# Hybrid mLSTM and short-convolution step: row operations in pieces inside the next pair, convolution ahead of the gates, chunks in two passes, four sums stored

## What is computed

```
xn = rmsnorm(x, norm_w)
q, k, v, i, f, o, z_m, b_g, c_g, x_c, z_c, g_m, g_c = split(xn @ w_in)      # 1024 x 10248
h  = mlstm_chunkwise(q, k * DQK**-0.5, v, i + b_i, log_sigmoid(f + b_f), C0, n0, m0)
h  = h * rsqrt(mean(h*h) + EPS) * head_norm_w
y_m = (h * sigmoid(o) * silu(z_m)) @ w_proj_m
y_c = (silu(z_c) * b_g * short_conv(c_g * x_c, conv0, conv_w)) @ w_proj_c
y  = rmsnorm(x + (sigmoid(g_m) * y_m + sigmoid(g_c) * y_c) @ w_out, final_norm_w)
```

## Time and profile before

| | us |
|---|---|
| three runs | 2537.21, 2540.91, 2544.01 (median 2540.91) |
| the profiled execution | 2534.89 |
| its span, first to last instruction | 2533.1 |
| TensorE busy in it | 2386.8 (94%) |
| DVE busy | 1556.8 (61%) |
| ACT busy | 886.8 (35%) |
| GpSimd busy | 95.2 (4%) |

### The profile page before, as it was taken

How to read it: one execution, slowest core, us unless ns; L and a number is a source line. 1 busy time by engine, 2 the same in 40 slices (tenths; PEclk the granted TensorE clock), 3 DMA queues, 4 the chain that set the end, 5 groups by cost and what they waited for, 6 DMA issues and landing times. The chain is left out here.

```text
span 2533.1 us, 42100 instructions
## 1 busy us (share of the span) xinstructions
PE 2386.8 (94%) x14825; PEld 2303.0 (91%) x14825; DVE 1556.8 (61%) x2792; ACT 886.8 (35%) x1613; POOL 95.2 (4%) x82
## 2 busy tenths in 40 slices
PE   7997998999998889999999899999998999999998
PEld 7996997999998889899999899998998999999886
DVE  4334777778887878666777766666776523333333
ACT  4223443443333434444344444443343301001111
POOL 0003000000000000000100000000000000000000
PEclk9998998999999889999999999999999999999999
DMA  6444766787755567566544446575542743335452
GB/s 208 125 125 130 266 201 220 248 241 225 255 198 195 177 234 229 188 208 197 187 154 160 145 159 209 173 220 171 145 155 103 257 154 110 99 95 173 126 148 84
DMA packets 303537, 449.50 MB, mean 177 GB/s; under 512 B 27226, under 2 KB 250586, under 8 KB 289622
## 3 DMA queue, kind: packets, MB, share of 16 engines
q1 hardware_dynamic: 303446, 448.31, 55.4%
HBM read 293.13 MB, written 155.16 MB: 177 GB/s over the span
## 5 line engine op out<-in xcount | busy, mean ns | idle before, releaser
L1453 PE MATMUL b_g<-x_hi,w_hi 128*128 128x344 f32 (+1 forms) x3024 | 999.3, 330 | 67.8 <-DVE part L1128 30.0
L1453 PE MATMUL b_g<-x_lo,w_hi 128*128 128x344 f32 (+1 forms) x3024 | 976.8, 323 | 0.0
L1453 PE MATMUL b_g<-x_hi,w_lo 128*128 128x344 f32 (+1 forms) x3024 | 974.7, 322 | 0.0
L1453 PEld LDWEIGHTS b_g<-x_hi,w_hi 128*128 128x128 f32 x3024 | 578.8, 191 | 81.9 <-DVE part L1128 29.3
L1453 PEld LDWEIGHTS b_g<-x_lo,w_hi 128*128 128x128 f32 x3024 | 579.2, 192 | 2.0
L1453 PEld LDWEIGHTS b_g<-x_hi,w_lo 128*128 128x128 f32 x3024 | 578.6, 191 | 0.0
L976 ACT ACTIVATE w_hi<-w_operands 128x512 fp32r<-128x512 f32 x533 | 332.9, 629 | 494.1 <-PE b_g L1453 488.1
L1095 DVE TENSOR_TENSOR w_lo<-w_operands,w_hi 128x512 fp32r<-128x512 f32 x533 | 373.3, 705 | 0.8 <-ACT w_hi L976 0.5
L1777 PE MATMUL c_g<-act_hi,RH 128*128 128x294 f32 x896 | 268.1, 299 | 11.7 <-DVE act_lo L1727 11.7
L1777 PE MATMUL c_g<-act_hi,RL 128*128 128x294 f32 x896 | 268.0, 299 | 0.0
L1777 PE MATMUL c_g<-act_lo,RH 128*128 128x294 f32 x896 | 267.5, 299 | 0.0
(11 more groups left out here) (257 smaller groups left out, 2548.7 us busy)
## 6 DMA issues: line engine op xcount, KB each, us to landing
w_operands<-w_ops_d SPq DMA_DIRECT2D x36, 1792.0 KB, 8.5
stages<-w_ops_d SPq DMA_DIRECT2D x36, 1024.0 KB, 5.1
w_ops_d<-w_operands SPq DMA_DIRECT2D x18, 1792.0 KB, 9.4
w_operands<-w_in SPq DMA_DIRECT2D x108, 256.0 KB, 4.8
w_operands<-w_ops_d SPq DMA_DIRECT2D x36, 768.0 KB, 7.3
w_ops_d<-stages SPq DMA_DIRECT2D x18, 1024.0 KB, 7.2
w_ops_d<-w_operands SPq DMA_DIRECT2D x18, 768.0 KB, 8.4
stages<-w_in SPq DMA_DIRECT2D x36, 256.0 KB, 3.7
```

The lines of the kernel that those rows point to most:

```text
L1453: last = nc.tensor.matmul(bank[:, 0:n], w[:, j, k, :], x[:, k, 0:n], start=(j < 4 and k == 0 and m == 0), stop=(k == 3 and m == 2), skip_g ...
```

## The change

Five things in phase b, and one in phase c.

1. `finish` is cut into pieces with a position `at`, and each engine issues piece j of the *previous* pair behind its step j of the current one (`ended`). The sums of the next-but-one pair move from steps 3 to 6 to steps 5 and 6 of the pair and 0 and 4 of the next. SP stores the odd pair's rows in the next body (`store_rows(*before, 1)`), and the weights after that.
2. The order is q/k, o/z, convolution, gates. The turn falls on the last gates body.
3. Chunks only in passes two (7) and three (9): convolution bodies 4 to 7, or 2 to 7, and gates 0 to 2. The decode's inputs are loaded in convolution body 1 of pass one, its rows written in body 2; four samples are updated in the o/z bodies of pass two and four in those of pass three, one per body; the next pass's x quarters are loaded in gates body 0.
4. `w_ops_d` holds the four sums only. A load in passes two and three is five transfers: three raw blocks from `w_in` and two of sums.
5. The first tap of the convolution (times `cw[2]`) and the eviction of each head's numerator go from DVE to ACT; DVE's multiplication by the head norm goes away, and phase c multiplies `w_proj_m` by it in the instructions that split it.

```diff
 def load_w(pair, p, s, i, q):                       # p > 0
-    src = g.w_ops_d[FIRST[s] + 2 * i + q]
-    for n, part in enumerate(g.W7[q]):
-        sp.dma_start(flat, src[:, 2048 * n:2048 * n + flat.shape[1]]).then_inc(w_ops_in[q], 16)
+    sp.dma_start(operand(g, q, 0), w[:, 0:4, c0:c0 + P]).then_inc(w_ops_in[q], 16)
+    sp.dma_start(operands(q, 1, 4), src[:, 0:3]).then_inc(w_ops_in[q], 16)
+    sp.dma_start(operand(g, q, 4), w[:, 4:8, c0:c0 + P]).then_inc(w_ops_in[q], 16)
+    sp.dma_start(operand(g, q, 5), w[:, 4:8, c1:c1 + P]).then_inc(w_ops_in[q], 16)
+    sp.dma_start(operand(g, q, 6), src[:, 3]).then_inc(w_ops_in[q], 16)
...
 # SP, one body
     load_w(pair + 2, *following, 0)
+    if extra == "chunk" and c not in (0, 7):
+        store_hg(c - 1)
+        load_gate(c)
+    if before:
+        store_rows(*before, 1)
     store_w(pair + 1, 1)                            # pass one
+    if extra == "chunk" and not last_chunk:
+        load_kq(c + 1)
...
     load_w(pair + 3, *following, 1)
-    store_w(pair + 2, 0)
     store_rows(p, s, i, 0)
+    store_w(pair + 2, 0)
...
-    store_rows(p, s, i, 1)
...
 # ACT, one body
     for q in range(2):
+        ended = (p, s, i, 0) if q else (*before, 1) if before else None
         for j in range(7):
             chunk(chunk_of(p, s, i), 7 * q + j)
             step(p, s, i, q, j)
-        finish(p, s, i, q)
+            if ended:
+                finish(*ended, j)                   # tanh at 0, gates' second tanh at 1
...
+    if s == "conv" and q == 0 and at == 1:
+        act.wait_ge(u_hist, 1 + 8 * p + i + 1)
+        nc.scalar.activation(CV[:, 0:n], UB[:, 2:2 + n], ACT.Copy, scale=cw[:, 2, bass.ds(i, 1)]).then_inc(cw_set, 1)
...
 def chunk(c, at):                                   # ACT, at 4, 6, 8, 10
+    act.wait_ge(den_set, NH * c + h + 1)
+    nc.scalar.activation(HB[:, h, :], PN[:, 0:DHV], ACT.Copy, scale=den[:, 1, h:h + 1]).then_inc(h_set, 1)
...
 # DVE, one body
         for j in range(7):
             extras(p, s, i, extra, 7 * q + j)
             step(p, s, i, q, j)
-            if s == "conv" and q == 1:
-                convolve(p, i, j)
-            if p == 0 and extra != "turn" and j >= 3:
-                sums(pair_of(p, s, i, q) + 2, half_of(p, s, i, q) + 1, q, j - 3)
+            if ended:
+                finish(*ended, j)
+            if p == 0 and not last_of_pass(s, i, q) and j in (0, 4):
+                sums(pair + 1, half + q, 1 - q, 2 if j == 0 else 3)
+            if p == 0 and extra != "turn" and j >= 5:
+                sums(pair + 2, half + 1, q, j - 5)
-        finish(p, s, i, q)
...
 # DVE's pieces: o/z at 1 (waits for z_set) and 2; the convolution's product at 0,
 # taps at 2, 3 and 4 (2 waits for cw_set); its three row operations at 1, 2 and 4
```

More of the change, by code:

```diff
@@ L581, in phase_b @@
[L581 to L584, removed]
+        [("qk", 0, 1, "gates_a"), ("qk", 1, 2, "gates_b"), ("oz", 0, 1, None), ("oz", 1, 4, None),
+         ("conv", 0, 1, "dec_inputs"), ("conv", 1, 2, "dec_first"), ("conv", 2, 3, "dec_rows"), ("conv", 3, 8, None),
+         ("gates", 0, 1, None), ("gates", 1, 3, None), ("gates", 3, 4, "turn")],
@@ new lines, in phase_b @@
+        [("qk", 0, 1, None), ("qk", 1, 2, None), ("oz", 0, 1, "decode"), ("oz", 1, 4, "decode"),
+         ("conv", 0, 1, None), ("conv", 1, 4, None), ("conv", 4, 8, "chunk"),
+         ("gates", 0, 1, "chunk"), ("gates", 1, 3, "chunk"), ("gates", 3, 4, "turn")],
+        [("qk", 0, 1, None), ("qk", 1, 2, None), ("oz", 0, 1, "decode"), ("oz", 1, 4, "decode"),
+         ("conv", 0, 1, None), ("conv", 1, 2, "dec_last"), ("conv", 2, 8, "chunk"),
+         ("gates", 0, 1, "chunk"), ("gates", 1, 3, "chunk"), ("gates", 3, 4, "end")]]
@@ new lines, in body @@
+                if extra == "decode":
+                    b = 4 * (p - 1) + i
+                    store_C(b)
+                    if i < 3:
+                        load_sample(b + 1)
+                if (p, s, i) in ((1, "conv", 3), (2, "conv", 1)):
+                    for par in range(2):
+                        sp.wait_ge(row_out[p][par], 1 + 16 * DMAS[p] * (2 * ROWS["qk"][par] + 4 * ROWS["oz"][par]))
+                    sp.wait_ge(state_out, 16 * (1 + 4 * p))
+                    first_loads(0 if p == 1 else 7)
@@ L1385, in extras, with body @@
                     ins.then_inc(ut_set, 1)
-            def body(p, s, i, extra):
+            def body(p, s, i, extra, before):
                 for q in range(2):
+                    ended = (p, s, i, 0) if q else (*before, 1) if before else None
+                    pair, half = pair_of(p, s, i, q), half_of(p, s, i, q)
                     for j in range(7):
@@ L1531, in extras @@
                     pe.wait_ge(dec_sq, 1)
[L1532 to L1533 removed]
+                    nc.tensor.matmul(PN[:, 0:2 * NS * NH], ones[:, :], dec[:, 3, :], start=True, stop=True).then_inc(dec_mm, 1)
+                elif extra == "end" and at == 2:
                     pe.wait_ge(c_set, HC + NH)
```

349 lines of the change are left out of this document (173 added, 176 removed).

## The result

The changed kernel takes 2467.7 us (median of four runs, 2466.9 to 2468.1) where the kernel before took 2542.0 beside it (2537.2 to 2544.0): a ratio of **0.971**, 95% interval 0.970 to 0.973. The prediction was 2472, range 2447 to 2512. The profiled execution took 2466.87 us, 68.0 less than the one of before. That the medians lie 74.3 apart is no second effect: the profile of before stood 7.1 under the 2542.0, that of after 0.8 under its own median.

The account below looks back on a forecast made before the run. Stalls of TensorE's projection products above undisturbed pairs, 140.1 us, were taken as what can be won, with VectorE late through a weight-load ring. Terms left 70.9, so 69.2 won: 2540.9 - 69.2 = 2472 us, range 2447 to 2512.

Parts of the forecast that it names:

- start: Start of the first pass: one weight sum fewer before it, stall 17.2 -> 16.5 us.
- o/z, first pass: Six o/z pairs of the first pass: earlier weight load and later sums cut the stall from 16.0 to 0.5 us.
- decode inputs: First-pass convolution body 1: TensorE waits for five loads, now also behind the row store; stall 10.7 -> 13 us.
- decode rows: First-pass convolution body 2: SP's wait for small stores delays the odd pair's load; stall 0 -> 3 us, bounds 0 and 8.
- two turns: Pass ends, now in gates pairs, where VectorE has 23 us against 13.2: both turns and q/k, 28.9 + 11.3 -> 13.0 us.
- o/z with decodes: O/z bodies of passes two and three, one decode each, late odd weights: 10.7 -> 5 and 0 -> 5 us.
- chunks: Chunk bodies of passes two and three: waits for scores and h, first loads and last decode; 5.1 + 11.4 -> 12.4 us.
- The ring: First pass: VectorE waits for the raw weight load, then late releases the next; earlier load and later sums end it.
- first loads and last decode: Part of the chunk term in passes two and three: +3 us.
- The later loads: Weight loads of passes two and three, five overlapping transfers: 10 us each, between 8.5 and 19; cover 12.8, with banks 15.2.
- slower rival: Five-part load misses quiet pairs too, lengthening all 72 pairs: +137 us, 2609 us; decides from 16.2 us of landing; 5%.
- scores late: Rival: VectorE comes late to the chunk's scores, ten convolution bodies pay 4.1 instead of 0.7 us: +34, 2506 us; 13%.

Follow-up runs that it names:

- the run with both edits undone: Changed kernel with row operations in one block behind their pair and the four weight sums early, both as before the change: 2574.7 us, ratio 1.015.
- the two single ones: Changed kernel with only the row operations in one block again (2517.6 us, ratio 0.992), and with only the four weight sums early again (2480.9 us, ratio 0.978).
- the run with the block: Changed kernel with a pair's row operations once more in one block behind its last step, in all bodies: 2517.6 us, ratio 0.992.
- the block in o/z: Changed kernel with row operations in one block behind their pair in o/z bodies alone, in pieces elsewhere: 2460.0 us, ratio 0.970.

## Why the prediction was right

The mechanism was right, and the total better than its terms: errors of both signs, 13.1 and 14.5 us, cancelled, and that is luck. By the terms 140.1 - 72.3 = 67.8 us were won where 69.2 were forecast; that the median came out 4 under the 2472 is no term of the sum. The forecast took the change from the profile off the median, as if the profile of after would lie 6.0 under its median too; it lies 0.8 under, which makes 5.2 us less, against 1.4 more in the terms. What stays, term by term as forecast and as measured from the windows above (the chunks with 1.9 of the last body):

| | forecast | measured |
|---|---|---|
| start | 16.5 | 14.8 |
| o/z, first pass | 0.5 | 0.0 |
| convolution and gates, first pass | 2.5 | 0.7 |
| decode inputs | 13 | 9.6 |
| decode rows | 3 | 0.0 |
| two turns | 13.0 | 10.9 |
| o/z with decodes | 5 + 5 | 4.4 + 5.0 |
| chunks | 12.4 | 26.9 |
| sum | 70.9 | 72.3 |

The 14.8 of the start are a matter of luck (about 17 in most of the runs). Two readings of the prediction were off, with little weight for the sum: by its own list 101.6 of the 140.1 us lay in the first pass and the turn behind it, not half, and of the two low halves stretched in the first turn only one took 3.45 us, the other 3.15.

**The ring** went as told, with slack on both sides: the run with both edits undone shows that it was the ring, and the two single ones that one half would have done in o/z. The prediction priced both together and didn't ask what each did alone.

**The chunks** are the mis-sized term, by 14.5 us. Three pieces of it. (1) 7.6: GpSimd's two x sums meet the chunk's decay. The prediction had this collision, with 5 us as its price, but in the turn pair, and left it out of the sum. It didn't ask when GpSimd would start: the sums have no wait of their own on the turn and follow GpSimd's last operation for the chunk, so they start right where VectorE needs the pair. (2) Ten convolution bodies at 37.3 and 37.1 instead of the 36.7 forecast. The piece ahead of the scores costs 0.79 (forecast 0.7, right); the other 0.5 a body was left out, and most of it is the 0.37 for the decay. VectorE comes to the sum of squares without a pause in these bodies, with the second tap and its addition just before it; that this is the cause is read from the timeline, no run moved the second tap. (3) What was forecast as first loads and last decode: 4.7 instead of 3. No wait for those loads is among TensorE's; 1.3 and 1.5 are matmuls of the first chunk and of the last decode in the windows without chunks, 1.9 lie in the last body. The gates bodies' wait for h was 0.2 to 0.4, as forecast.

**The decode's inputs.** The wait was 4.9, not 8. The queue was as told (the row store goes at 444.1, 10.3 us into the body, and the five loads behind it; the two runs with a later row store wait 8.1 and 8.2), but not its speed. SP's queue, start and length of the issues, from the first of the five loads to the last:

```profile
446.07 0.90 SPq L795 DMA_DIRECT2D gate<-qT_d  x1
...
449.32 0.81 SPq L803 DMA_DIRECT2D v_ones<-v_rows  x1
```

4.1 us from the first issue to the end of the last; in the kernel before the same five took 8.0 (776.95 to 784.99), two of them 2.35 and 2.79 us, behind a store of 1.75 MB. The run that stores all seven operands has the order of the changed kernel and a store of 1.75 MB: 5.7 us (448.10 to 453.83), and TensorE waits 6.5. So the smaller store accounts for 1.6 of the 3.9 us; the rest stays open. With no store ahead of them at all, in the run that loads the inputs first, they take 3.9 (440.48 to 444.37). The prediction added the queue's order and took its speed over.

**The decode's rows** cost nothing, for the same reason. SP's 9.7 us for its small stores were not the stores' own price:

```profile
486.40 0.98 SPq L811 DMA_DIRECT2D fir_d<-sample_small  x3
488.69 0.35 SPq L813 DMA_DIRECT2D sample_wide<-fir_d  x1
```

1.3 us from the last of them to the reload, 4.6 from the first (484.11). In the kernel before it was 11.9 from the first (814.65), and a 1.75 MB load and a 1.75 MB store stood just ahead of them in the queue (the parts of such a store landed in 7.2 and 8.4 us in the median); here only a store of 1.0 MB does, whose parts land in 3.5 and 3.9. The run with all seven operands stored takes the store by itself: 1.75 MB stand ahead again, without the load (its parts land in 4.1 and 5.5), the first small store goes at 487.30, and then

```profile
490.70 1.29 SPq L804 DMA_DIRECT2D fir_d<-sample_small  x3
493.49 0.34 SPq L806 DMA_DIRECT2D sample_wide<-fir_d  x1
```

which is 6.2 us from the first and 1.5 from the last. So the store's size accounts for 1.6 of the 7.3 us. That most of the rest was the large load beside it is what is left to suspect; no run has that load alone.

**The later loads**, in five parts, came down in 8.3 us in the median (the last part goes 2.0 behind the first and lands 6.3 later), where the prediction took 10 between 8.5 and 19; in o/z bodies with a decode some took longer, for one 10.7 (from SP's first issue at 840.40 to 851.09, where ACT, which had stood 3.34 for it, goes on). So the slower rival, which needed 16.2, never had its condition: the parts overlap. The Trainium skill spoke for that rival ("DMA: Bandwidth & Descriptors", "Rules for kernel authors": join small transfers). The run with all seven stored agrees in kind, with 7.9 us for one transfer of the same bytes and 7.3 for two; but the undisturbed pairs are no longer by it.

**The decodes** came out as forecast (9.4 against 10) and by the forecast mechanism, ACT's tanh behind the late weights: the block in o/z takes it away whole.

Of the rivals, "scores late" was real as a mechanism and is what the run with the block shows, at 5.3 us a body and not 3.4, with h late behind it and the clock at 0.95. Of the signs named in advance three were missed, all by terms above: the chunk bodies behind convolution (37.3 and 37.1, forecast 36.5 to 37), the wait for the decode's inputs, and the first pass, which came out 31 us over its undisturbed pairs and not 40. Those that would have spoken against it stayed clear: 26.4 us for the body with the decode rows (32), 37.3 for the chunk bodies (40).

## What to carry to other kernels

A ring is opened by either end of it; undo the halves one by one before you pay for both. Here late sums alone would have opened it; the pieces cost 0.8 us per chunk behind convolution and 9 in the decodes and bought nothing in the ring, and it is elsewhere, in the chunk bodies, that they earned 50. Where a piece of work goes in an in-order queue decides its price: the same 0.93 us tap cost under 0.1 us of TensorE's wait behind the operation that starts another engine's turn, 1.0 ahead of it (by the timeline, not by a run of its own), and held the next chunk's first operation back by 1.5 us where it stood ahead of that. When work moves, ask what its engine does just before it and who shares a port or a queue with it there, not only whether it fits in the sum.

## What was not expected of the hardware

GpSimd's large additions stop even short SBUF operations of VectorE: four of 128 columns took 6.46 us instead of 0.87; its power of 128x4 stopped nothing. A small transfer has no fixed price: from the last of the same six small stores to the reload SP waited 9.7 us in one kernel, 1.3 in the other, and 1.5 with a store of 1.75 instead of 1.0 MB ahead of them. And 245 instead of 186 GB/s on the DMA queues changed nothing in a stretch of six pairs, 79.1 us against 79.0.
